# Routings split at their links among dot products and attention, second-table rows spread over query jobs: a one-layer decoder step with 16,384 experts on one core

## What is computed

```python
q = (xb @ w_q).reshape(TOK_BLK, PEER_HEADS, 2, DK_HALF)
s = jnp.einsum('thcd,hcnd->thcn', q, sub_keys).astype(jnp.float32)
s1, i1 = lax.top_k(s[:, :, 0], TOPK)
s2, i2 = lax.top_k(s[:, :, 1], TOPK)
cand = (s1[..., :, None] + s2[..., None, :]).reshape(TOK_BLK, PEER_HEADS, TOPK * TOPK)
cid = (i1[..., :, None] * N_KEYS + i2[..., None, :]).reshape(TOK_BLK, PEER_HEADS, TOPK * TOPK)
top_s, pos = lax.top_k(cand, TOPK)
eid = jnp.take_along_axis(cid, pos, axis=-1)
g = jax.nn.softmax(top_s, axis=-1).astype(xb.dtype)
hid = jax.nn.gelu(jnp.einsum('thkd,td->thk', u_tab[eid], xb), approximate=False)
return jnp.einsum('thk,thkd->td', g * hid, v_tab[eid])
```

## Time and profile before

| | us |
|---|---|
| median of 3 runs | 2047.26 (2037.34 to 2053.65) |
| the profiled execution | 2047.33 |
| its span on the core | 2045.5 |
| TensorE / VectorE / ScalarE / GpSimd busy | 1513.8 / 1087.3 / 215.8 / 1044.0 |
| moved by DMA | 670 MB, mean 328 GB/s |

### The profile page before, as it was taken

One profiled execution on the slowest core, in us unless ns is written; L12 is line 12 of the kernel. 1 busy time (PEld: TensorE's weight loads), 2 busy tenths in 40 slices (PEclk: granted clock), 3 DMA queues, 4 the chain that ended last, 5 costly groups with the idle time before them and its releaser, 6 DMA issues.

```text
span 2045.5 us, 16501 instructions
## 1 busy us (share of the span) xinstructions
PE 1513.8 (74%) x5398; PEld 547.7 (27%) x5398; DVE 1087.3 (53%) x2879; ACT 215.8 (11%) x610; POOL 1044.0 (51%) x1119
## 2 busy tenths in 40 slices
PE   7889977678977777775666676665666666777997
PEld 4475644444432223431111111111111111111221
DVE  2257868783356545526655556666666666422000
ACT  2411123343100000010100000010000000100000
POOL 3032332341555546346566666665555556666664
PEclk9799997778999889898899999998999888899999
DMA  9587868998998779769799999997888889999997
GB/s 320 198 315 253 310 248 328 343 405 329 332 385 329 279 282 377 297 230 377 288 369 372 357 368 357 360 382 284 325 317 321 323 319 339 342 367 363 370 363 280
DMA packets 213254, 670.00 MB, mean 328 GB/s; under 512 B 19600, under 2 KB 54656, under 8 KB 213040
## 3 DMA queue, kind: packets, MB, share of 16 engines
q0 software_dynamic: 157728, 571.78, 74.0%
q1 hardware_dynamic: 55440, 97.16, 13.3%
HBM read 663.26 MB, written 5.60 MB: 327 GB/s over the span
## 4 chain that ended last, share of the span: by engine, by line
PE 28%; DVE 19%; issue 16%; DMA 15%; POOL 14%; another core or an unknown queue 5%; ACT 2%; DVEq 0%; SPq 0%; ACTq 0%; POOLq 0%
POOL area_r L1576 14%; PE bank L774 10%; PE bank L549 6%; DMA area_r<-in_v_tab,eidT 6%; DMA area_r<-in_u_tab,eid 6%; DVE area_r L1431 6%; PE bank L719 3%; PE bank L672 2%; DMA area_w<-in_v_cache 2%; DVE area_w L1360 1%; DVE area_w L1358 1%; DVE rt L1361 1%; PE bank L492 1%; DVE rtu L1331 1%
## 5 line engine op out<-in xcount | busy, mean ns | idle before, releaser
L774 PE MATMUL bank<-area_r,area_c 128*32 128x512 f32 (+1 forms) x1632 | 697.5, 630 | 253.8 <-DMA area_r<-in_v_tab,eidT 223.1
L1431 DVE CUSTOM_DVE_ANT_0 area_r<-area_r,bank 128x1024 f32<-128x1024 f32 x544 | 648.0, 1217 | 423.3 <-DMA area_r<-in_u_tab,eid 364.4
L1576 POOL DMA_INDIRECT area_r<-in_u_tab,eid x544 | 515.1, 947 | 616.1 <-DVE hid L1431 381.1
L1576 POOL DMA_INDIRECT area_r<-in_v_tab,eidT x544 | 513.4, 944 | 369.9 <-PE bank L774 153.4
L774 PE MATMUL bank<-area_r,area_v 128*32 128x512 f32 (+1 forms) x544 | 285.1, 650 | 119.1 <-DMA area_r<-in_v_tab,eidT 107.2
L774 PEld LDWEIGHTS bank<-area_r,area_c 128*32 128x32 f32 (+1 forms) x1632 | 136.8, 111 | 788.3 <-DMA area_r<-in_v_tab,eidT 464.0
L549 PE MATMUL bank<-area_w,area_t 128*128 128x384 f32 (+1 forms) x448 | 160.8, 515 | 12.7 <-issue 8.5
L719 PE MATMUL bank<-area_t,area_w 128*128 128x128 f32 (+2 forms) x672 | 134.0, 360 | 22.6 <-ACT area_x L878 19.3
L774 PEld LDWEIGHTS bank<-area_r,area_v 128*32 128x32 f32 (+1 forms) x544 | 51.1, 114 | 312.5 <-DMA area_r<-in_v_tab,eidT 197.1
L719 PEld LDWEIGHTS bank<-area_t,area_w 128*128 128x128 f32 x672 | 101.9, 203 | 54.2 <-issue 42.6
L549 PEld LDWEIGHTS bank<-area_w,area_t 128*128 128x128 f32 x448 | 85.3, 194 | 78.8 <-issue 29.7
(11 more groups left out here) (168 smaller groups left out, 1006.2 us busy)
## 6 DMA issues: line engine op xcount, KB each, us to landing
area_w<-in_w_q SPq DMA_DIRECT2D x21, 1024.0 KB, 8.0
area_w<-in_w_in SPq DMA_DIRECT2D x12, 1536.0 KB, 10.5
area_w<-in_k_cache SPq DMA_DIRECT2D x8, 1920.0 KB, 19.2
area_w<-in_v_cache SPq DMA_DIRECT2D x8, 1920.0 KB
area_r<-in_u_tab,eid POOLq DMA_INDIRECT x544
area_r<-in_v_tab,eidT POOLq DMA_INDIRECT x544
area_w<-in_w_out SPq DMA_DIRECT2D x4, 2048.0 KB, 9.6
area_w<-in_w_in SPq DMA_DIRECT2D x2, 2048.0 KB, 14.3
```

The source lines that it names most:

```text
L774: mm = pe.matmul(acc[CG * g:CG * g + m, e, :], wd[g][:, c * CG:c * CG + m], v_ring[s][:, e * 512:(e + 1) * 512], start=False, stop=False, ...
L1431: vec.tensor_tensor_reduce(out=u_ring[s], in0=u_ring[s], in1=x_cur, scale=1.0, scalar=0.0, op0=ALU.mult, op1=ALU.add, accum_out=hid[t % 2] ...
L1576: nc.gpsimd.indirect_dma_start(out=ring[s], out_offset=None, in_=table, in_offset=bass.IndirectOffsetOnAxis(ap=where, axis=0)).then_inc(la ...
```

## The change

`route(k)` becomes a generator. Its instructions, their order and its twelve waits stay; behind each link it hands control back (`yield`), and the wait for that link stands at the start of the next piece, so other instructions can stand between a link and its wait. `go_on(links, n)` runs up to n pieces. A routing is 13 pieces with the last wait and the writing of the numbers.

- Routing 1 goes piecewise into the first 12 dots (0 still stands ahead of them).
- Projection: routings 2, 3, 4, 5 from units 3, 9, 15, 21, one piece before and one after each dot.
- Attention: routings 6 and 7 from groups 1 and 7, a piece at each `between` and one behind each dot; 3 dots at `between(i, 1)` ahead of each sample group, in place of 5 ahead of those whose group had no routing.
- Steps 8 to 30: pieces only behind the 4th to the 16th dot of a step, one per dot (two per dot in steps with two routings, one routing after the other). A routing so begins behind dot 4 (before: 8, or 5 and 10) and writes its numbers behind the step's last dot (in steps with two: the first behind the 10th, the second behind the 16th). 8 and 9 stay a block.
- `queries(i, tokens)` takes a pair: 4 and 4 rows at jobs 13, 15, 17, 19, 4 and 0 at jobs 14, 16, 18, 20. `EID_FIRST` goes from 104 to 108, `EID_AT` from 92 to 98.

```diff
-ROUTE_PROJ = {4: 2, 11: 3, 18: 4}
-ROUTE_ATT = {1: 5, 4: 6, 10: 7}
+ROUTE_PROJ = {3: 2, 9: 3, 15: 4, 21: 5}
+ROUTE_ATT = {1: 6, 7: 7}
-EID_AT = 92
-EID_FIRST = 104
+EID_AT = 98
+EID_FIRST = 108
-            return 5 if before and i - NG0 not in ROUTE_ATT else 0
+            return 3 if before else 0
@@ queries
-                    weigh_first(tokens)
+                    weigh_first(tokens[c])
-            queries(EARLY_END, 4)
+            queries(EARLY_END, (4, 4))
-                    queries(i + 1, 4 if made[0] + 8 <= EID_FIRST else 0)
+                    queries(i + 1, (4, 4) if (i - EARLY_END) % 2 else (4, 0))
@@ route, the same at each of the twelve links
-                link(ins)
+                ins.then_inc(route_link, 1)
+                yield
+                linked(1)
@@ new
+            def routings(ks):
+                for k in ks:
+                    if k % HEADS == 0 and 2 * HEADS <= k:
+                        finish_gates(k // HEADS - 1)
+                    yield from route(k)
+                    if k == HEADS * NT - 1:
+                        finish_gates(SAMP)
+                    yield
+            def go_on(links, n=HEADS * NT * LINKS):
+                for _ in range(n):
+                    if next(links, SLOTS) == SLOTS:
+                        break
@@ projection
-                    route(ROUTE_PROJ[u - NC])
-                dots_to(dots_by_unit(u))
+                    go_on(links)
+                    links = route(ROUTE_PROJ[u - NC])
+                while made_dots[0] < dots_by_unit(u):
+                    go_on(links, 1)
+                    dots_to(made_dots[0] + 1)
+                    go_on(links, 1)
@@ attention, experts_between
-                if j == 1 and i - NG0 in ROUTE_ATT:
-                    route(ROUTE_ATT[i - NG0])
+                if j == 0 and i - NG0 in ROUTE_ATT:
+                    go_on(links[0])
+                    links[0] = route(ROUTE_ATT[i - NG0])
+                go_on(links[0], 1)
-                dots_to(min(made_dots[0] + dots_in_group(i, j), SLOTS))
+                for _ in range(dots_in_group(i, j)):
+                    dots_to(min(made_dots[0] + 1, SLOTS))
+                    go_on(links[0], 1)
@@ steps of tiles 1 to 4
-                    for i, k in enumerate(ks):
-                        dots_to(g * TOPK + (i + 1) * TOPK // (len(ks) + 1))
-                        ...
-                        route(k)
-                        ...
-                    dots_to((g + 1) * TOPK)
+                    links = routings(ks)
+                    for i in range(TOPK):
+                        dots_to(g * TOPK + i + 1)
+                        if i >= TOPK - LINKS - 1:
+                            go_on(links, len(ks))
+                    go_on(links)
```

## The result

| | before | after | ratio, 95% interval |
|---|---|---|---|
| median of runs | 2046.61 us (4 runs, 2037.34 to 2053.65) | 1922.24 us (4 runs, 1917.76 to 1933.13) | 0.9403 [0.9347, 0.9459] |
| profiled execution | 2047.3 us | 1924.79 us | |
| its span | 2045.5 us | 1923.0 us | |

The account below looks back on a forecast made before the run. DMA's 1.28 us per gather set each stage's floor, with POOL's in-order waits above it. Terms -10 (ahead of stage 1), -38, -29 and -62 (stages 1 to 3) made -139 from 2047.3: 1908 us, range 1870 to 1980.

Parts of the forecast that it names:

- Stage 3, -47 for -62: Stage 3 (tile 3): routings in pieces end POOL's waits for VectorE, 420 to 358 us, -62; ends 345 and 413.
- the 38 us of waits left over: Stage 3: waits expected to remain, taken from stage 2 of before, 24.2 for TensorE and 13.9 without a releaser.
- the 41 to 46 us: Stage 3: sign that a step with two routings, 52.7 us before, would take 41 to 46 us.
- Stage 2, -14 for -29: Stage 2 (tile 2): 23 us of VectorE waits and some of TensorE's 24.2 go, 379 to 350 us, -29.
- The end "379": Stage 2: slow end of the forecast's range, 379 us, no gain; the other end was 339.
- they come from thirty instructions in a row into a full queue: Gaps of 2 to 2.6 us before VectorE's routing instructions: the reading the forecast took, by which single pieces hide them.
- they belong to the instructions: The other reading of VectorE's gaps: two-routing steps cost 50.8 us and the seven steps 24 to 30 win nothing.
- rival 2: Steps with routings: gaps stay with the pieces, stage 3 gives -7 in place of -62, 1963 us in all; chance 0.13.
- Rival 1: Stages: DMA's 413 GB/s doesn't last, whole stages stay at 356; stage 2 gives 0, stage 3 -37, 1962 us; chance 0.16.
- The new wait: Ahead of tile 2: routing 16's numbers come behind dot 16 of step 15, so POOL stands some 5 us, once.
- Stage 1, -42.5 for -38: Stage 1 (tile 1): rows over query jobs and routings in pieces, 401 to 363 us, -38; ends 348 and 386.
- Ahead of stage 1, -16.5 for -10: Projection and attention: pieces between dots give -3 and -7, in sum -10; ends 0 and -18.

Follow-up runs that it names:

- set 3: On one chip: the change (1924.83 us), before (2049.05), the changed kernel with gathers of 2 KB (1908.32) and without the work of routings 16 to 39 (1911.34).
- set 1: On one chip: the changed kernel with one part undone at a time (1852.83, 1838.00, 1815.39 us) or without routing work from 16 on (1801.28); before 1883.94.
- half rows: The changed kernel with gathers of 2 KB per partition in place of 4 and dots adding in place of multiplying: 1908.32 us.
- set 2: On one chip: the change (1929.74 us), before (2050.36), the changed kernel with stage 1's two waits taken away (1923.81) and without routings' counting instructions (1925.58).

## Why the prediction came out as it did

**The direction and the mechanism held.** POOL waited in order for dots behind whole routings, and pieces end that: its waits for VectorE went from 100.3 to 14.8 us in stage 3 (the prediction said under 25) and from 23.0 to 5.3 in stage 2. The share of DMA is 0.97 in both, as it said (0.95 or more).

**Stage 3, -47 for -62: the term that was too small is the 38 us of waits left over.** It took them from stage 2 of before, 24.2 for TensorE and 13.9 without a releaser. After, 13.9 are for TensorE, 30.8 without a releaser and 14.8 for VectorE, 59.5 in sum. Before, stage 3 showed a single stop without a releaser, 4.4 us; I read it so that the others fell into POOL's waits for VectorE and came out when these went; that is argued, but without routings on VectorE stage 3 still has 52.4 us of waits. The two kinds that the term added up, TensorE's and those without a releaser, were probably for the most part one kind, the stops that come every 24 gathers or so (set 3). On set 1's chip, which has no such stops, the stage is 339 us and the two-routing steps take 41.5 to 44.5 us, inside the 41 to 46 us that the prediction named; on the chip of the result they take 41.2 to 55.2, 47.8 on average (before: 52.9), so that sign failed there.

**Stage 2, -14 for -29: the same term.** VectorE's waits fell by 17.7 of the 23.0 counted, but TensorE's rose by 3.4, where I had 6 us of them go with the waits for VectorE. They didn't: on another such chip stage 2 stands at 365.8 without any routing work. The end "379" of its range was nearer than the end "339".

**The gaps of VectorE.** The prediction chose between "they come from thirty instructions in a row into a full queue" and "they belong to the instructions". Neither is right. In pieces they are as many and longer, 32 with 99.2 us against 30 with 70.6, so rival 2's premise came true. Its consequence didn't: a gap ahead of one piece now holds back one dot, with six buffers to cover it, not a dot behind a whole routing. And they don't belong to the instructions, since another chip has none. So the choice on which the forecast stood failed, and the time came out near all the same: the prediction had the gaps go with the blocks, but they stayed, and what went was most of their effect (that the six buffers cover it is argued). What gaps cost a kernel is where the difference shows: on set 1's chip pieces were worth 29 us in stage 3; the whole change is worth 47 there on the chip of the result.

**Rival 1** (the rate doesn't last) described the chip of the result halfway: 366 to 371 GB/s at a share of 0.97, which its sign (a rate under 370 at a share near 1) half meets, and 30.8 us without a releaser in stage 3, which is under the 40. Its reason is not a limit of DMA, as the 403 to 409 GB/s of set 1 and the half rows of set 3 show.

**The new wait** came as told: one wait of POOL for `eid` ahead of tile 2, forecast at 5 us. POOL's timeline after:

```profile
898.06 0.94 POOL L1626 DMA_INDIRECT area_r<-in_u_tab,eid  x1 [5.51 <-DVE eid L1388]
```

**Stage 1, -42.5 for -38.** POOL's longest wait for TensorE is 8.2 us, from 31.2; the prediction said none over 10 (the change in set 2 has one of 11.97). Routing 13's wait for scores moved and didn't go, as told, and grew. VectorE's timeline:

```profile
701.38 0.49 DVE L1326 MAX8 rt<-area_w 128x8 f32<-128x128 f32 x2 [20.00 <-ACT area_w L878]
```

It was 15.39. POOL pays 11.63 us for it (in its timeline at 703.26). The rest of the stage was forecast as its floor of 311 times 1.15; on set 1's chip it is 327.

**Ahead of stage 1, -16.5 for -10.** The term for attention was too small: DMA's share was capped there by 0.96, but a share of 1.02 is to be had. Over its stretch the rate rose from 361 to 396 GB/s, and its end came 18.0 us sooner (dot 127 at 459.3, before 477.3), 7 of which were already won in projection (dot 68 at 296.2, before 303.1). The "7 us at most" for attention should have been made from the best short rate, 413 GB/s, not from a share of 1: 177 us x (1 - 361 / 413) = 22.

Two terms too large by 30 us and two too small by 11, with 2.7 at the end: 139 - 30 + 11 + 2.7 = 122.7. The errors of the terms partly cancel, so the sum is better than its parts: the 1922 for 1908 is in part luck. So is the chip, since on one like set 1's there would have been no gaps or stops to forecast.

## What to carry to other kernels

Where one queue issues transfers for two consumers in order, the longest unbroken piece of work between two uses of a buffer sets its waits: cut such work at its own dependencies and lay it between the uses, even if nothing of it gets shorter. Sum the waits of the issuing engine by stage before and after; what is left over in them is the next question. List them in order as well: waits at one pace under changing names are one thing. A rate or a gap read in one profile may belong to one chip: run the kernel before again beside every experiment, and let a forecast say which of its terms rest on an unexplained gap, because work that hides a gap hides it on one chip and finds none on the next.

## What the runs showed of the hardware

Chips differ far more than runs. The same kernel before took 1884 us on one chip and 2047 to 2050 in three comparisons elsewhere (medians; lowest and highest of those 2035 and 2060). The profiles show what goes with it: idle times of mostly 1.2 to 6 us ahead of VectorE's instructions and of 2 to 5 us ahead of POOL's gathers, which no work of the kernel explains, on these; none on the first, in any of the four kernels profiled there (their lists of POOL's waits name no other releaser than VectorE, TensorE and its own queue). The change is worth 6% where the stops are. On the chip without them it wasn't run; from the kernel with blocks ahead of stage 1 (1815.4) less the 12 us of that part it would be about 1803, and from the kernel without routing work (1801.3) plus the 5.5 us of that work about 1807: 4% under 1884. Those are estimates.

What the stops are stays open. Shown is what they are not. POOL's stay with half the bytes and DMA at a share of 0.65, so they are not a full queue, which the prediction suspected for VectorE's gaps (those stay too, 41 with 132 us), and they stay with no routing on VectorE. Shown too is their pace in stage 2, one in about 24 gathers or 34 us, most regular where no routing work is in the way. In the change of set 3 they stand closer behind stage 3, ahead of gathers 940, 958 and 976, 18 apart (26 us), where two second-table gathers stand to one of the first. Both distances are 12 second-table gathers, twice round that table's six buffers. Why that should stop POOL on one chip and not on another no run shows; another number of buffers would test it. The supply of instructions was hardly changed by any run (37 to 44 packets in that queue), and is untested as their cause. That VectorE's gaps and POOL's stops have one cause is a guess: fewer than half of them end together.
